# Where the convolution taps of a decoder layer stand on VectorE

## The reference

```
h = rmsnorm(x)
q_m,k_m,v_m,i,f,o, glu_a,glu_b, q_a,k_a,v_a, g = split(h @ w_in)
y_a = (sigmoid(o) * mLSTM(q_m,k_m,v_m,i,f)) @ w_mlstm_out
u   = glu_a * sigmoid(glu_b)
uc  = causal_dwconv(u, 31 taps) + b
y_b = silu(layernorm(uc)) @ w_conv_out
y_c = windowed_attention(rope(q_a), rope(k_a), v_a, sinks) @ w_attn_out
x  += (g_a*y_a + g_b*y_b + g_c*y_c) @ w_out
x  += ConvFFN(rmsnorm(x))
```

## Time and profile before

| | us |
|---|---|
| median of 3 runs | 1043.05 (1042.21 to 1044.66) |
| the profiled execution | 1041.96 |
| its span, first to last instruction | 1039.8 |
| TensorE busy | 1004.8 (97%) |
| VectorE busy | 770.2 (74%) |
| ScalarE busy | 571.8 (55%) |
| GpSimd busy | 39.9 (4%) |

### The profile page before, as it was taken

The page is one execution under the profiler, slowest core; times in us unless marked ns, Lnnn a source line. Parts: engine busy times, 40 slices in busy tenths (PEclk is TensorE's granted clock), DMA queues, the critical chain, the costliest instruction groups (busy, mean ns, idle before and its releaser), DMA issues.

```text
span 1039.8 us, 19576 instructions
## 1 busy us (share of the span) xinstructions
PE 1004.8 (97%) x7896; PEld 959.4 (92%) x7896; DVE 770.2 (74%) x1475; ACT 571.8 (55%) x1079; POOL 39.9 (4%) x55
## 2 busy tenths in 40 slices
PE   4999999999999999999979999999999999999997
PEld 3999989988999999999979998898899999999997
DVE  4577897876787877775574879978678877887563
ACT  4545665646646655553344465657466655665542
POOL 0011000021000000000000200000210000000000
PEclk9999999999999999999989999999999999999998
DMA  9754546456545765555487546363755667666552
GB/s 237 179 146 128 128 116 163 124 140 173 159 138 163 233 199 168 170 165 172 148 194 162 147 128 143 104 180 103 184 167 165 166 165 243 182 183 178 171 171 76
DMA packets 318659, 167.92 MB, mean 161 GB/s; under 512 B 25294, under 2 KB 317502, under 8 KB 318506
## 3 DMA queue, kind: packets, MB, share of 16 engines
q1 hardware_dynamic: 318426, 165.87, 58.3%
q10 hardware_dynamic: 144, 0.80, 0.2%
HBM read 160.11 MB, written 9.71 MB: 163 GB/s over the span
## 4 chain that ended last, share of the span: by engine, by line
PE 83%; DVE 6%; ACT 5%; DMA 3%; issue 2%; SPq 0%; DVEq 0%
PE ps_tile L949 17%; PE ps_tile L950 16%; PE ps_tile L951 16%; PE work L949 7%; PE work L951 7%; PE work L950 7%; DMA w_raw<-in_w_in 2%; DVE w_lo L1883 2%; ACT w_hi L1359 1%; ACT scores L1515 1%; PE work L1183 1%; PE work L1185 1%; PE work L1193 1%; PE work L1167 1%; DVE prod L1940 1%
## 5 line engine op out<-in xcount | busy, mean ns | idle before, releaser
L1883 DVE TENSOR_TENSOR w_lo<-w_raw,w_hi 128x1024 fp32r<-128x1024 f32 (+1 forms) x288 | 343.1, 1197 | 99.5 <-ACT w_hi L1359 98.6
L1359 ACT ACTIVATE w_hi<-w_raw 128x1024 fp32r<-128x1024 f32 (+1 forms) x288 | 295.3, 1028 | 148.6 <-DMA w_raw<-in_w_in 65.9
L949 PE MATMUL ps_tile<-h_hi,w_hi 128*128 128x280 f32 (+2 forms) x944 | 282.8, 300 | 9.1 <-DVE h_lo L1893 8.9
L950 PE MATMUL ps_tile<-h_lo,w_hi 128*128 128x280 f32 (+2 forms) x944 | 275.7, 292 | 0.0
L951 PE MATMUL ps_tile<-h_hi,w_lo 128*128 128x280 f32 (+2 forms) x944 | 275.3, 292 | 0.0
L949 PEld LDWEIGHTS ps_tile<-h_hi,w_hi 128*128 128x128 f32 (+1 forms) x944 | 178.4, 189 | 15.3 <-issue 13.0
L950 PEld LDWEIGHTS ps_tile<-h_lo,w_hi 128*128 128x128 f32 (+1 forms) x944 | 178.4, 189 | 1.1
L951 PEld LDWEIGHTS ps_tile<-h_hi,w_lo 128*128 128x128 f32 (+1 forms) x944 | 178.0, 189 | 0.6
L949 PE MATMUL ps_tile<-xg_hi,w_hi 128*128 128x280 f32 (+2 forms) x368 | 106.4, 289 | 0.3 <-DVE w_lo L1883 0.3
L951 PE MATMUL ps_tile<-xg_hi,w_lo 128*128 128x280 f32 (+2 forms) x368 | 105.8, 287 | 0.0
L950 PE MATMUL ps_tile<-xg_lo,w_hi 128*128 128x280 f32 (+2 forms) x368 | 105.8, 287 | 0.0
(11 more groups left out here) (377 smaller groups left out, 1822.3 us busy)
## 6 DMA issues: line engine op xcount, KB each, us to landing
w_raw<-in_w_in SPq DMA_DIRECT2D x98, 512.0 KB, 3.9
w_raw<-in_w_ffn_gate SPq DMA_DIRECT2D x44, 512.0 KB, 3.9
w_raw<-in_w_ffn_up SPq DMA_DIRECT2D x44, 512.0 KB, 3.9
w_raw<-in_w_ffn_down SPq DMA_DIRECT2D x32, 512.0 KB, 3.6
w_raw<-in_w_out SPq DMA_DIRECT2D x16, 512.0 KB, 3.7
w_raw<-in_w_ffn_down SPq DMA_DIRECT2D x14, 384.0 KB, 3.2
w_raw<-in_w_in SPq DMA_DIRECT2D x20, 256.0 KB, 3.6
c_head<-in_state_mlstm_c SPq DMA_DIRECT2D x8, 512.0 KB, 5.6
```

The lines of the kernel that those rows point to most:

```text
L949: mm(out, hi[:, k, :], a_hi[:, k0 + k, f:T], start=first, stop=False, skip_group_check=True)
L950: mm(out, hi[:, k, :], a_lo[:, k0 + k, f:T], start=False, stop=False, skip_group_check=True)
L1359: go(h, r, ACT.Copy).then_inc(w_hi_ready, 1)
L1883: tt(lo, r, h.bitcast(F32), ALU.subtract).then_inc(w_split[n % SLOTS], 1)
```

## The change

Three things are changed. The table of taps begins at step 5 instead of 8, with new counts. The order of taps is no longer round the chunks from a finished last chunk: a planner, tap_order, takes in each step the chunk with the fewest taps done, among those whose gated input was made in an earlier step. A tap 0 waits for its own chunk's input, and a later tap for the tap before it in the same chunk. And in VectorE's steps the lower half of a block is put ahead of the division.

The number of taps by step, before and now: 5 to 7 none, now 2, 3, 3; 8 and 9 four each, now five; 10 two, now three; 11 to 13 four, now six; 14 to 21 as before; the even steps 22 to 36 four, now two; the odd steps 21 to 35 two as before; 37 to 46 as before; 47 five, now four. 124 in both.

```
-CONV_FROM, CONV_TO = 8, 49
-BUSY = {10: 2, 14: 0, 15: 0, 16: 3, ...
+CONV_FROM, CONV_TO = 5, 49
+BUSY = {5: 2, 6: 3, 7: 3, 8: 5, 9: 5, 10: 3, 11: 6, 12: 6, 13: 6, **{n: 2 for n in range(22, 37, 2)}, 14: 0, ...
+def tap_order():
+    order, done = [], [0] * KC
+    for n, count in enumerate(TAPS_AT):
+        for _ in range(count):
+            open_chunks = [c for c in range(KC) if STEP["glua", c] < n and done[c] < CONV_W]
+            if open_chunks:
+                c = min(open_chunks, key=lambda c: (done[c], c))
+                order.append((n, done[c], c))
+                done[c] += 1
+    assert len(order) == KC * CONV_W
+    return order
+TAPS = tap_order()
+TAP_NO = {(tap, c): i for i, (_, tap, c) in enumerate(TAPS)}
...
-                def taps(first, count):
-                    for i in range(first, min(first + count, KC * CONV_W)):
-                        tap, c = divmod(i, KC)
+                def taps(n):
+                    for at, tap, c in TAPS:
+                        if at != n:
+                            continue
...
                         if tap == 0:
-                            if c == 0:
-                                dve.wait_ge(took_dve, value("took_dve", l, DVE_NO["glua", KC - 1] + 1))
+                            dve.wait_ge(took_dve, value("took_dve", l, DVE_NO["glua", c] + 1))
...
-                            dve.wait_ge(tap_done, value("tap_done", l, i - KC + 1))
+                            dve.wait_ge(tap_done, value("tap_done", l, TAP_NO[tap - 1, c] + 1))
...
+                    if n - 1 in VALUES_AT[1::2]:
+                        block_att_lo(VALUES_AT.index(n - 1) // 2)
                     if n - 2 in SCORES_AT:
                         softmax_unit_2(SCORES_AT.index(n - 2))
                     if n == 22:
                         sample_att_lo()
-                    if n - 1 in VALUES_AT[1::2]:
-                        block_att_lo(VALUES_AT.index(n - 1) // 2)
```

More of the change, by code:

```diff
@@ L222 @@
 UNITS = [(blk, pair) for blk in range(3) for pair in range(2)]
-CONV_FROM, CONV_TO = 8, 49
-BUSY = {10: 2, 14: 0, 15: 0, 16: 3, 17: 1, 18: 1, 19: 0, 20: 1, 37: 5, 38: 5, 39: 0, 40: 3, 41: 1, 42: 5,
+CONV_FROM, CONV_TO = 5, 49
+BUSY = {5: 2, 6: 3, 7: 3, 8: 5, 9: 5, 10: 3, 11: 6, 12: 6, 13: 6, **{n: 2 for n in range(22, 37, 2)}, 14: 0, 15: 0, 16: 3, 17: 1, 18: 1, 19: 0, 20: 1, 37: 5, 38: 5, 39: 0, 40: 3, 41: 1, 42: 5,
         **{n: 6 for n in range(43, 49)}, **{n: 2 for n in range(21, 37, 2)}}
@@ L1978, in take @@
                         tt(merged[:, t, f:T], old, prod[:, t % 2, f:T], ALU.add).then_inc(merged_ready, 1)
-                def taps(first, count):
-                    for i in range(first, min(first + count, KC * CONV_W)):
-                        tap, c = divmod(i, KC)
-                        w, dst, src = vcol("w_dconv", i), uc[:, c, 0:NP], u_pad[:, c, tap:tap + NP]
+                def taps(n):
+                    for at, tap, c in TAPS:
+                        if at != n:
+                            continue
+                        w, dst, src = vcol("w_dconv", tap * KC + c), uc[:, c, 0:NP], u_pad[:, c, tap:tap + NP]
                         if tap == 0:
-                            if c == 0:
-                                dve.wait_ge(took_dve, value("took_dve", l, DVE_NO["glua", KC - 1] + 1))
-                                dve.wait_ge(pad_zero, value("pad_zero", l, 1))
-                                dve.wait_ge(vec_ready, value("vec_ready", l, 2))
+                            dve.wait_ge(took_dve, value("took_dve", l, DVE_NO["glua", c] + 1))
+                            dve.wait_ge(pad_zero, value("pad_zero", l, 1))
+                            dve.wait_ge(vec_ready, value("vec_ready", l, 2))
                             ts(dst, src, w, vcol("b_dconv", c), ALU.mult, ALU.add).then_inc(tap_done, 1)
                         else:
-                            dve.wait_ge(tap_done, value("tap_done", l, i - KC + 1))
+                            dve.wait_ge(tap_done, value("tap_done", l, TAP_NO[tap - 1, c] + 1))
                             stt(dst, src, w, dst, ALU.mult, ALU.add).then_inc(tap_done, 1)
@@ L2317, in _ @@
                         decayed_scores(ML_AT.index(n))
-                    taps(sum(TAPS_AT[:n]), TAPS_AT[n])
+                    taps(n)
             last = D_MODEL - P
```

## The result

The changed kernel takes 1049.86 us (median of 5 runs, 1049.52 to 1051.56) where the kernel before took 1043.05 beside it (5 runs): the ratio is 1.0067, with a 95% interval of 1.0056 to 1.0079. The forecast was 1045.0 with a range up to 1047.3: the sign is right, the size is not, and the time lies outside the range. The profiled execution took 1049.86 us with a span of 1047.5.

The account below looks back on a forecast made before the run. The prediction took TensorE, in order and busy for 97% of the span, as the bound. Rope waits of + 3.98 us less 2.02 for the swap gave + 1.96 on the median 1043.05: 1045.0 us, range 1042.2 to 1047.3.

Parts of the forecast that it names:

- Ten taps in steps 5 to 9 for nothing: Before piece 14's split: ten added taps, 4.1 us, fit into VectorE's 8.4 us of idle and cost nothing.
- Seven taps, 2.87 us on the rope: Steps 10 to 13: VectorE has no slack, so seven added taps of 0.41 us delay everything up to the rope.
- That the taps and splits in a row hold it: GpSimd's first cosine product stays held until the gate bias; TensorE's new rope waits, 1.75 and 2.23 us, make 3.98 us.
- the sum: Whole execution: + 3.98 us for the rope less 2.02 for the swap, + 1.96 us.
- GpSimd gets in early: Rival at the rope: GpSimd's first product is done when the rope starts, so + 1.24 us, 1044.3 us; chance 0.10.
- The swap: Attention, step 29: value products slide under the division, winning 1.01 us a layer, 2.02 us together.
- The waits of 0.8 in layer 1 and some 0.5 at the turning: Signs in the attention: TensorE waits about 0.8 us for layer 1's lower half and about 0.5 for the division.
- a late upper half in the attention: Rival: ScalarE's upper half comes late, so the swap wins nothing, 1047.0 us; chance 0.12.
- the slower rival: The rival of the late upper half in the attention: swap wins nothing, 1043.05 + 3.98 = 1047.0 us; chance 0.12.

Follow-up runs that it names:

- the two runs where the taps did hold the product: The changed kernel with twelve taps in step 13 (ratio 1.0027), and the changed kernel with GpSimd's first cosine product waiting for step 13's third tap (1.0011).
- the run: The kernel before, with only the lower half put ahead of the division: ratio 0.9969 to the kernel before (0.9958 to 0.998), 3.2 us won.
- the same kernel: The changed kernel with GpSimd's first cosine product waiting for the first of step 13's six taps: ratio 1.0055 to the kernel before (1.0034 to 1.0076).

## Why the prediction was wrong

- **Ten taps in steps 5 to 9 for nothing: right.** VectorE still idles 2.83 us before the split of piece 14, and TensorE's wait for a split is 0.3 us as before.
- **Seven taps, 2.87 us on the rope: right as a term.** With GpSimd kept out the gate bias is 2.91 us later.
- **"That the taps and splits in a row hold it, that it runs when the gate bias does, and that the rope keeps its shape and shifts as a whole: 3.98 us." This step failed.** It read the 2.54 us of the earlier trace rows as what a row of taps does to GpSimd, without asking in which tap the product would be queued once VectorE runs later. It was queued a split earlier, and five products took turns with five taps: 2.7 us more on VectorE in each layer, in part given back by a rope of 85.59 + 0.45 − 81.76 = 4.28 us instead of 5.09. TensorE waited 7.7 us where 3.98 stood in the sum. Taking GpSimd out of the taps brought the ratio from 1.0067 to 1.0037. In the two runs where the taps did hold the product as the prediction assumed, the ratio was 1.0027 and 1.0011, on either side of the forecast's 1.0019. That closeness is in part luck: their rope waits were 2.8 and 2.9 us and not 3.98, and both have two stretches of half clock, which the sum did not have.
- **The rival "GpSimd gets in early" named the event and gave it the wrong sign.** It counted what an early product saves the rope, 0.36 us a layer (0.81 in the trace, 5.09 less 4.28), and not the 2.7 that the products take from the taps beside them.
- **The clock had no term.** Behind waits of 3.6 and 4.0 us the granted clock was 0.5. The trace of before has no wait at this place, and behind the one of 2.4 us in the attention its clock stayed at 1.00. But it has one of the length in question at the start of layer 1, just behind another of 1.7 us, and the clock behind it is at half. The prediction did not look there (list of waits from 510 to 560 us, then the stretch behind the longer wait):

```profile
PE ps_tile L949 <- DVE h_lo L1893: 3.7, 1, 3.7
```
```profile
536.80:543.00 6.20, 6.20 (x27) 6.20 (x28) 5.56 (x14) 4.18 (x8) 0.00 (x0) 0.52 1.09 227
```

Filling the long wait gave back 2.6 us, and filling the shorter ones 3.9.
- **The swap: right in mechanism, small in size.** 2.02 forecast, 2.5 by the changed trace's waits, 3.2 by the run. The waits of 0.8 in layer 1 and some 0.5 at the turning came as written (0.8 and 0.37). The run's interval begins at 2.1, just above the forecast.
- **The range ended too low** since its upper end was a late upper half in the attention; no case had two costs at once in the stretch where VectorE had no slack. Nor does 1047.3 follow from its own words: the slower rival's 1047.0 and a scatter of 1.6 us above it make 1048.6, which is still too low.

By the changed trace the sum of + 1.96 becomes + 9.1: 3.7 more of wait for the rope (7.7 for 3.98) and 3.9 for the clock, less 0.5 for the larger swap. The other shifts named above take 1.4 of it back in that execution, and 7.7 us of span are left. The runs give 7.0 us in all: 3.1 go when GpSimd is kept out of the taps (1.0067 to 1.0037), some of the clock among them since the waits become shorter, and 3.9 more when the waits are filled (1.0037 to 1.0000). Each of these steps carries an interval of over 1 us.

## What to carry to other kernels

When instructions are added to a stretch in which another engine's work slows this one's, ask not only how much later the point comes but which instruction will be running when the other engine's work is queued: by that alone the same five products cost VectorE 0.8 us (in the rope) or 2.7 us (in the taps) a layer. A transfer of work into a stretch with no slack is better put in front of it, where 2.8 us of idle stood open. Price a new wait of several us at more than its length where TensorE's clock may fall behind it, and look for the price at a wait of that length anywhere in the trace.

## What was not expected of the hardware

- A two-input VectorE tap of 0.41 us pitch beside a waiting GpSimd product runs at 0.95 once they take turns; held, the product can last 5.44 us instead of 0.77.
- Whether it is held can differ between two layers of one execution (3.69 us and 0.93 us in the same kernel).
- Behind a TensorE wait of 3.6 to 4.0 us the granted clock was 0.5 for 3.4 and 6.8 us; a stretch of 3.4 us also came where TensorE had no listed wait in the 26 us ahead.
